# Router fed by the raw residual, pairwise ranks, counts ahead of gate products, and expert weights held for two gathers

## What is computed

```python
x  = x + gate1 * mixed                              # mixed = merged @ w_o
h2 = rms_norm(x, norm2_g) * (1 + scale2) + shift2
gl = h2 @ w_rg + b_rg ; el = (h2 @ w_re + b_re)     # 4 group logits, 4x4 expert logits
g  = top1(softmax(gl)) ; e1, e2 = top2(softmax(el[g]))
out = sum over the two picks of weight * (silu(h2 @ w_e_gate) * (h2 @ w_e_up)) @ w_e_down
y  = rms_norm(x + gate2 * out, norm_final_g)
```

## Time and profile before

| | us |
|---|---|
| median of 3 runs (734.41 to 739.53) | 736.75 |
| time of the profiled execution | 738.45 |
| its span in the trace | 736.6 |
| PE busy in the span | 701.6 (95%) |
| DVE, ACT, POOL busy | 539.6, 346.0, 213.6 |
| last unit of the projection ends | about 507.0 |
| `slot_i` complete | 532.5 |
| first expert product starts | 542.8 |
| one expert slot in the steady stretch | 9.34 |

### The profile page before, as it was taken

How to read it: one execution, slowest core, us unless ns; L and a number is a source line. 1 busy time by engine, 2 the same in 40 slices (tenths; PEclk the granted TensorE clock), 3 DMA queues, 4 the chain that set the end, 5 groups by cost and what they waited for, 6 DMA issues and landing times.

```text
span 736.6 us, 11162 instructions
## 1 busy us (share of the span) xinstructions
PE 701.6 (95%) x4432; PEld 614.1 (83%) x4432; DVE 539.6 (73%) x782; ACT 346.0 (47%) x457; POOL 213.6 (29%) x89
## 2 busy tenths in 40 slices
PE   5899999999999999999999999999789999998984
PEld 2499999999998898999999999887368888887862
DVE  3547999999758765865466564556689999988976
ACT  4552223433333443455366031124368888777643
POOL 4004322222200000000000000000129999899475
PEclk9999999999999999999999999999789999999998
DMA  9954145545624446431234334274948999989874
GB/s 324 377 168 142 58 172 172 172 172 174 215 86 66 76 119 127 58 119 58 79 100 135 105 112 176 85 280 172 420 154 335 398 406 408 419 325 396 309 247 181
DMA packets 75607, 149.10 MB, mean 202 GB/s; under 512 B 11302, under 2 KB 54626, under 8 KB 68836
## 3 DMA queue, kind: packets, MB, share of 16 engines
q1 hardware_dynamic: 61572, 125.28, 49.7%
q10 hardware_dynamic: 10096, 12.63, 4.8%
q0 software_dynamic: 3888, 10.49, 4.2%
HBM read 138.29 MB, written 20.05 MB: 215 GB/s over the span
## 4 chain that ended last, share of the span: by engine, by line
PE 76%; DMA 8%; DVE 4%; issue 4%; POOL 3%; ACT 2%; SPq 2%; POOLq 0%; DVEq 0%; ACTq 0%
PE psum L1009 36%; PE psum L1260 8%; PE psum L1302 7%; DMA down_raw<-in_w_e_down 3%; PE psum L514 3%; PE psum L515 3%; PE psum L520 3%; PE psum L944 3%; DMA w_more<-in_w_ada 2%; PE psum L1207 2%; DMA xg<-h_d,slot_b 2%; PE psum L1028 1%; SPq L807 1%; PE psum L1137 1%; PE psum L1144 1%
## 5 line engine op out<-in xcount | busy, mean ns | idle before, releaser
L1009 PE MATMUL psum<-hh,w_h 128*128 128x320 f32 x608 | 145.0, 320 | 0.2 <-issue 0.2
L1009 PE MATMUL psum<-hh,w_l 128*128 128x320 f32 x608 | 138.8, 310 | 0.0
L1009 PE MATMUL psum<-hl,w_h 128*128 128x320 f32 x608 | 138.7, 309 | 0.0
L2036 DVE SCALAR_TENSOR_TENSOR psum<-conv,taps,psum 128x760 f32<-128x760 f32 x103 | 104.5, 1015 | 3.5
L1009 PEld LDWEIGHTS psum<-hh,w_h 128*128 128x128 f32 x608 | 100.2, 189 | 5.4 <-issue 3.1
L1009 PEld LDWEIGHTS psum<-hl,w_h 128*128 128x128 f32 x608 | 102.0, 188 | 0.0
L1009 PEld LDWEIGHTS psum<-hh,w_l 128*128 128x128 f32 x608 | 101.8, 188 | 0.0
L692 POOL TENSOR_TENSOR ob<-obh,toff 128x260 bf16<-128x260 f32 x1 | 2.0, 1994 | 333.4 <-DVE obh L600 333.4
L726 POOL TENSOR_TENSOR down_l<-down_raw,down_h 128x2048 fp32r<-128x2048 f32 x16 | 88.4, 5522 | 19.6 <-ACT down_h L1804 19.2
L2322 DVE TENSOR_TENSOR w_l<-w_raw,w_h 128x2048 fp32r<-128x2048 f32 x26 | 75.8, 2917 | 11.3 <-ACT w_h L1810 11.3
L936 POOL TENSOR_TENSOR w_l<-w_raw,w_h 128x2048 fp32r<-128x2048 f32 x9 | 41.7, 4636 | 144.0 <-ACT w_h L1485 144.0
(11 more groups left out here) (385 smaller groups left out, 1411.2 us busy)
## 6 DMA issues: line engine op xcount, KB each, us to landing
w_raw<-in_w_in SPq DMA_DIRECT2D x20, 1024.0 KB, 14.4
down_raw<-in_w_e_down SPq DMA_DIRECT2D x17, 1024.0 KB, 12.2
w_raw<-in_w_ada SPq DMA_DIRECT2D x16, 1024.0 KB, 9.0
w_raw<-in_w_e_gate SPq DMA_DIRECT2D x13, 1024.0 KB
w_raw<-in_w_e_up SPq DMA_DIRECT2D x13, 1024.0 KB, 11.3
w_more<-in_w_ada SPq DMA_DIRECT2D x8, 1024.0 KB, 10.4
y_d<-yy ACTq DMA_DIRECT2D x15, 512.0 KB
y_d<-in_x_sample SPq DMA_DIRECT2D x12, 512.0 KB
```

What stands on the lines that cost most here:

```text
L1009: mm = pe.matmul(psum[:, p + q, 0:HALF], w, r[:, k, q * HALF:(q + 1) * HALF], start=(k == 0 and x == 0), stop=(k == KT - 1 and x == 2))
L2036: ins = dve.scalar_tensor_tensor(out=after, in0=src, scalar=w, in1=before, op0=MUL, op1=ADD)
```

## The change

- The turns take raw `x2` instead of `h2`, in halves of 512 columns; `1 + scale2` with the norm's weight goes into the router's weights (`wrs`, two sets), `shift2` into a row added at the end (`shw`, `lgc`), and the root mean square is applied to the logits (`scaled_logits`). `wr` is laid out in another order, so it is loaded in four pieces, and four small column loads are added.
- Three tiles are turned inside the projection's second half; tiles 0 and 1 get their logits, picks, counts and places there as well.
- The picks come from pairwise comparisons (`choose`): 16 differences for each set of four, a comparison, a sum.
- POOL makes seven half-tile products for `h2` (the left half of all, the right half of tiles 0 and 1); DVE's last operation makes the rest.
- Slot numbers come from sums of indicator products instead of a scan over rounded blocks, and the slot table from `oav`, which carries the token number, so that one product of 26 columns does it.
- The first gate2 product stands ahead of the late counts and the second behind them; the last two stand behind the slot table's product. `keep_clock` loops of 8, 3 and 3 go, one of 4 stays.
- Slot 0's high products start when the first half of the tokens is ready; the table of weights, one gate2 spread and the turn of slot 1's tokens stand behind them.
- The last tile of `h2` is stored by POOL's queue. SP issues down weights of slot 0 after the logits, gate and up weights of slot 2 after the second gather has landed, down weights of slots 1 and 2 after the weights' table (`rt_pe` 4). The load of the final norm's weight (512 KB) moves into slot 2.

```diff
@@ choose and scaled_logits, in place of routing @@
+            ins = dve.scalar_tensor_tensor(out=lg[:, t, :], in0=psum[:, 7, LG_AT[t]:LG_AT[t] + 20],
+                                           scalar=rms[:, 24 + t:25 + t], in1=lgc[:, min(t, 1), :], op0=MUL, op1=ADD)
...
+        then(dve.tensor_tensor(ahead, sets.unsqueeze(2).to_broadcast(wide), sets.unsqueeze(3).to_broadcast(wide), SUB))
...
+        then(dve.tensor_reduce(rank[:, 0:n, :, :].rearrange("p t s e -> p (t s) e"), ahead, AX, ADD))
+        then(dve.tensor_scalar(ghot[:, 0:n, :], rank[:, 0:n, 0, :], 0.0, None, ALU.is_equal))
@@ experts_pool @@
-        pool.wait_ge(picked, 2)
-        pool.tensor_tensor(ob[:, :, :, 1, :], obh[:, :, :, :], toff[:, :, :].unsqueeze(1).to_broadcast([P, 2, NT, NS]),
-                           MUL).then_inc(consts, 1)
-        pool.wait_ge(h2_st, 16 * (NT + 1))
+        pool.wait_ge(mod_in, 16 * 6)
+        for t in range(NT):
+            pool.wait_ge(x2_left, X2_LEFT + t + 1)
+            pool.tensor_tensor(h2[:, t, 0:512], x2[:, t, 0:512], bsc[:, min(t, 1), 0:512], MUL).then_inc(h2_half, 1)
+        for t in range(ROUTED):
+            pool.wait_ge(x2_done, t + 1)
+            pool.tensor_tensor(h2[:, t, 512:D], x2[:, t, 512:D], bsc[:, min(t, 1), 512:D], MUL).then_inc(h2_half, 1)
+        pool.wait_ge(h2_dve, NT)
+        pool.dma_start(h2_d[(NT - 1) * P:NT * P, :], h2[:, NT - 1, :]).then_inc(h2_last_st, 16)
+        pool.wait_ge(h2_last_st, 16)
+        pool.wait_ge(h2_st, 16 * NT)
         pool.wait_ge(slots, 1)
@@ SP @@
         gate_up(1, 1, own(1))
-        for t in range(3, NT):
-            h2_store(t)
+        h2_store(3)
+        sp.wait_ge(lg_done, 2)
+        down_weights(0, 0, own(0))
+        sp.wait_ge(xg_in[1], 16)
         gate_up(2, 0, own(2))
-        sp.wait_ge(x2_done, NT)
+        sp.wait_ge(h2_st, 16 * NT)
+        sp.wait_ge(h2_last_st, 16)
+        sp.wait_ge(rt_pe, 4)
         down_weights(1, 1, own(1))
-        sp.wait_ge(lg_done, 1)
-        down_weights(0, 0, own(0))
-        sp.wait_ge(h2_st, 16 * (NT + 1))
         down_weights(2, 0, own(2))
@@ PE, inside the projection @@
+                    if half and t == ROUTED + 1 and k == 1:
+                        pe.wait_ge(lgc_done, LGC_DONE)
+                        for early in range(ROUTED):
+                            last = token_logits(early)
+                        last.then_inc(lg_done, 1)
+                    if half and 1 <= t <= ROUTED and k == 4:
+                        turn_x2(t - 1, 0)
+                        turn_x2(t - 1, 1)
+                    if half and t == NT - 1 and k == 2:
+                        early_counts()
+                    if half and t == NT - 1 and k == 5:
+                        turn_x2(2, 0)
+                        turn_x2(2, 1)
@@ PE, slot 0 @@
+            if first:
+                pe.wait_ge(e_hi, 2)
+                for k in range(KT):
+                    if k % 4 == 0:
+                        pe.wait_ge(x_lo, k // 4 + 1)
+                    for x in (xh, xl):
+                        pe.matmul(psum[:, s, :], x[:, s, k, :], both(wh, k), start=(k == 0 and x is xh), stop=False)
+                row_weights()
+                gate2_spread(1)
+                turn_x(1 - s, u + s, b + 1)
@@ DVE, between the halves of the projection @@
+        dve.wait_ge(late_in, 16 * 6)
+        dve.wait_ge(cols_in, COLS_IN + 16 * 4)
+        for v in range(2):
+            dve.tensor_tensor(wrs[:, v, :, :], wr[:, :, :], scol[:, v, :].unsqueeze(2).to_broadcast([P, KT, GRP]), MUL)
@@ DVE, ahead of slot 0 @@
-        for c in range(2):
-            w_lo(0, 0, c)
+        w_lo(0, 0, 0)
         x_low(0, 0, 0)
         x_low(0, 0, 1)
+        w_lo(0, 0, 1)
         late_tables(dve, then)
+        weight_table(dve, then)
```

549 lines of the change are left out of this document (368 added, 181 removed).

## The result

The changed kernel takes 740.8 us (median of 20 runs, 737.47 to 743.62) against 737.9 for the kernel before in the same session (734.41 to 743.13): ratio 1.0034, 95% interval 1.0019 to 1.0049. The medians lie 2.9 us apart; the ratio, which I use from here on, makes it 2.5 us, less than 1%. The forecast was 732.4 us with a range of 727 to 738, so the time lies outside it, on the slower side. It had been counted from 736.75 us, the median of only 3 runs of the kernel before.

A forecast was written before the change was run, and what follows sets the result against it. A chain through DVE, ACT, PE and the first gather binds ahead of slot 1; then PE, later DMA and POOL. -7.9 + (9.4 - 10.3) + (11.5 - 7.65) = -5.0; +0.6 gives -4.4: 732.4 us from 736.75, range 727 to 738.

The forecast's parts named there:

- The projection, +2.2 us: Projection on PE: 2.2 us longer from added turns, logits, sums and counts, ending near 509.2.
- rival 3: Projection's second half: POOL's operations lock DVE out and PE stops mid-unit; slower, 740 us; chance 0.08.
- Projection's end to logits, 5.2 us: Projection's end to DVE's scaled logits: 5.2 us instead of 11.8, since turns need x2 only.
- Logits to `slot_i`, 10.2 us: Routing on DVE: 10.2 us instead of 13.7, slot_i complete at 524.6 instead of 532.47.
- `slot_i` to the first product, 9.4 us: slot_i through the first gather to slot 0's first product: 9.4 us instead of 10.3, product at 534.0.
- The sentence on what would make me wrong: Wrong if PE idles over 1 us in the projection, first gather or last store lands after 531, or slots 3 to 12 lengthen.
- First product to slot 1, 11.5 us: Slot 0's first product to slot 1's turn of act: 11.5 us instead of 7.65, starting at 545.5.
- What the slots give back, 0.6 us: Expert slots: 0.6 us lost, half the 1.3 us of the norm weight's load in the saturated stretch.
- rival 2: Late slots: DMA and POOL hold the end and take back slot 1's lead; gain 1 us, 735.7; chance 0.2.
- The held loads: Ahead of slot 1: 4 MB of slots 1 and 2 weights fill nearly idle DMA from 531 to 544, costing nothing.
- The clock: Slot 0's products: half clock at first, 4.0 us taken for 16; all at half clock about 3 us worse, 735.4.
- forecast 5.0: Slot 1's first turn of act on PE: 5.0 us earlier, at 545.5 instead of 550.47.

The follow-up runs named there:

- i1: g4 with the turn of x2's tile 2 moved from inside the projection's last unit to behind the projection; ratio 1.0026 to the kernel before.
- g4: f4 with the end part's third sum of gathered rows moved from POOL to DVE; ratio 1.0002 to the kernel before.
- e2: Changed kernel with h2's last tile stored by SP's queue, ahead of 3 MB of expert weights; ratio 1.0010 to the kernel before.
- e1: Changed kernel with h2's last tile stored on ACT's queue instead of POOL's; ratio 1.0044 to the kernel before.
- f3: e2 plus slot 1's first low part ahead of x_low and the third gate2 product ahead of the slot table; ratio 1.0005 to the kernel before.
- f4: f3 plus six clock-keeping rows on PE in its end-part wait for POOL's third sum; ratio 1.0000 to the kernel before.
- g1 to g3: Kernel before, changed kernel and f4, each with slot result stores cut to 32 KB and y_d filled early; 738.19, 738.13 and 734.36 us.
- e3: Changed kernel with slot 2's pair and down weights issued once h2 is stored, ahead of the gather; ratio 1.0079 to the kernel before.

## Why the prediction was wrong

- **The projection, +2.2 us:** it is +2.9, the same 60.16 to 60.18 us in 12 of the 14 other traces with the change, less only in i1 and 0.26 more in g4. Durations of short products were underestimated. PE had no idle time in it, so rival 3 did not happen. POOL and DVE do hold each other up: POOL's half product beside DVE's `w_l` (467.67, 2.28 us) took 3.28 us instead of 1.30, and DVE's adds took 1.34 and 1.07 instead of 0.69, and the units' buffering took all of it, as forecast.
- **Projection's end to logits, 5.2 us:** 5.85. **Logits to `slot_i`, 10.2 us:** 9.97. These two steps, the core of the change, are right within 0.7 us: `slot_i` was forecast for 524.6 and is complete at 525.5, 7 us earlier than before.
- **`slot_i` to the first product, 9.4 us:** 12.3. This step failed. I took the last store as about 4 us, with the DMA queues near their end at 524, and started the gather 0.95 us behind `slot_i`. The store took 8.81 us. The 5.5 MB in front of it were not through at 524 either: the last load of them landed at 529.0, and the share was still 1.01 in 524 to 526. I gave the loads' end time to the gather and not to the store in front of it. The sentence on what would make me wrong had the place right: the first gather landed at 533.8, behind 531. The kernel before had shown the price. For `h_d` in 505 to 540, its trace says of the last two stores of `h2`, both on SP's queue behind the same kind of loads:

```profile
DMA to landing us min/median/max: 12.1/12.3/12.5
```

  e2 shows that the loads ahead delay the store, and e1 excludes POOL's queue. Of the 2.9 us in this step the store explains 1.9 (first product 26.2 us behind the projection's end in e1 and e2, 28.1 in the changed kernel); 1.06 of it as PE's wait for the gather, the rest because the clock came back 27.7 us behind the projection's end instead of 25.2. The other 1.0 is PE's own path, which I had right in its order and too short in its price: the slot table's product took 2.31 us, the turn 1.97 and the spread 2.75, all at half clock. The gather itself, forecast 4 us, took 4.39.
- **First product to slot 1, 11.5 us:** 11.6, with `act` 2 us behind `sil` in DVE's queue, as worked out.
- **What the slots give back, 0.6 us:** 1.6 us on 0.7 us of lead, and more on larger leads. I had rival 2 for it at 0.2 with a gain of 1 us left. Its mechanism is real and stronger than priced: f3 and f4 keep nothing of 2.1 and 2.5 us. A sum that ends at slot 1 was the wrong sum. The held loads did not fill 531 to 544 either: slot 2's pair went out at 536.9, the down weights of slots 1 and 2 at 542.5 and slot 3's pair at 547.0, all into one full stretch. A slot of 9.34 us asks for four times 1024 KB, 4.19 million bytes or 449 GB/s, and the full stretches show 381 to 420 with the share at 1.01: the reserve of loaded buffers is eaten up slot by slot, as the landing times and g1 to g3 show, and the earlier trace rows hinted at it. Behind it POOL and DVE add the round of 10.33 us. What the end of f4's lead owes to each of the two was not separated.
- **The end part:** not in the forecast at all, +2.5 us in the trace, 1.6 of them clock.
- **The clock:** the rule on HAM oscillation in the Trainium skill (TensorE: Matmul & The Clock Gate), that gaps ahead of products are paid for again, agrees with two places in the traces, slot 1 in e1 to e3 and the end part, where the clock falls some 1 us behind a wait of 2.1 to 2.5 us; the same waits in other traces do not drop it. The fall at 520.3 does not follow from the wait of 2.80 us, which had just begun. I had priced the clock at one place, and PE ran at half clock from 520.3 to 537.4.

The sum of the misses, in one pair of traces: 0.7 us in the projection, 3.6 from its end to slot 1 (2.9 of them the failed step), 1.0 in the slots and 2.5 in the end part, 7.8 us between -4.4 and +3.4. So the failed step alone does not turn the gain into a loss. That slot 1 still starts 0.7 us earlier than before is what is left of the forecast 5.0.

What is open: the ratio puts the changed kernel 2.5 us above before; the projection's 2.9 us, slot 1's gain, the slots and the end part add up to 3.4 in one pair of traces, but how the end part's share spreads over executions was not measured. Why the reserve is used up one or two slots sooner with the change than before is not tested either. No version here with full traffic beats the kernel before: f4 and g4 equal it.
